# Transformer front end as a stream: modulation blocks grouped by chunk of h, first two projection blocks summed side by side

## What is computed

```python
sh1, sc1, g1, sh2, sc2, g2 = split(silu(cond) @ w_ada + b_ada, 6)   # 6 x 1024 for each of two conditions
h = rms_norm(x, norm1) * (1.0 + sc1) + sh1
z = h @ w_in                 # q | k | v | conv_in, 1792 wide
attn = attention(q, k, v)    # windowed, grouped heads, rotary, sink
conv = conformer_conv(u)     # GLU -> depthwise conv of 31 taps -> LayerNorm -> swish -> pointwise
x = x + g1 * (concat(attn, conv) @ w_out)
h2 = rms_norm(x, norm2) * (1.0 + sc2) + sh2
x = x + g2 * peer(h2)        # 16384 one-neuron experts, top 16 of each of 8 heads
```

## Time and profile before

| | |
|---|---|
| time, three runs | 1817.09 us median (1816.93 to 1817.82) |
| time of the profiled execution | 1817.6 us |
| its span, first to last instruction | 1815.6 us |
| mean granted clock of TensorE | 0.966 of full speed |
| TensorE matmul busy | 1692.0 us, 93% |
| VectorE busy | 1577.9 us, 87% |
| ScalarE busy | 767.1 us, 42% |
| GpSimd busy | 686.8 us, 38% |
| first part of the modulation and the norm, up to the first projection matmul | 0 to 38.3 us |
| input projection | 38.3 to 196.7 us |

### The profile page before, as it was taken

How to read it: one execution, slowest core, us unless ns; L and a number is a source line. 1 busy time by engine, 2 the same in 40 slices (tenths; PEclk the granted TensorE clock), 3 DMA queues, 4 the chain that set the end, 5 groups by cost and what they waited for, 6 DMA issues and landing times.

```text
span 1815.6 us, 28944 instructions
## 1 busy us (share of the span) xinstructions
PE 1692.0 (93%) x9360; PEld 1420.6 (78%) x9360; DVE 1577.9 (87%) x3181; ACT 767.1 (42%) x1653; POOL 686.8 (38%) x611
## 2 busy tenths in 40 slices
PE   6999988999963887799999999999999999999997
PEld 4566766955542787699989999998999999999986
DVE  2687852488889997799999999999999999999998
ACT  3122563330002888344444444444444444444443
POOL 0000000035565887344344444434343444444441
PEclk9999999999885999899999999999999999999999
DMA  8443102211112478999999999999999999999996
GB/s 318 140 142 137 47 1 73 70 59 58 35 35 93 140 228 256 367 398 388 392 405 400 400 401 398 414 390 394 408 406 395 409 393 404 404 410 399 394 392 211
DMA packets 128781, 508.71 MB, mean 280 GB/s; under 512 B 8528, under 2 KB 63568, under 8 KB 79312
## 3 DMA queue, kind: packets, MB, share of 16 engines
q0 software_dynamic: 36864, 268.45, 36.8%
q1 hardware_dynamic: 91568, 239.34, 35.2%
q10 hardware_dynamic: 288, 0.13, 0.0%
HBM read 479.97 MB, written 27.92 MB: 280 GB/s over the span
## 4 chain that ended last, share of the span: by engine, by line
DVE 35%; DMA 23%; PE 21%; issue 18%; POOL 1%; ACT 1%; DVEq 1%; POOLq 0%; SPq 0%; ACTq 0%
DMA slab<-table,ixr 21%; DVE slab L1452 8%; PE psum L413 7%; DVE ulo L1368 4%; PE psum L619 3%; DVE slab L1406 3%; DVE slab L1444 3%; PE psum L706 2%; DVE vlo L1431 2%; PE psum L414 2%; DVE slab L1439 2%; DVE wlo L1427 1%; POOL slab L1534 1%; PE psum L550 1%; DVE slab L1410 1%
## 5 line engine op out<-in xcount | busy, mean ns | idle before, releaser
L1534 POOL DMA_INDIRECT slab<-table,ixr x256 | 426.0, 1664 | 604.0 <-DVE slab L1452 554.3
L727 PE MATMUL psum<-hhi,uhi 128*128 128x384 f32 x1008 | 340.1, 337 | 7.4 <-issue 7.1
L1452 DVE SCALAR_TENSOR_TENSOR slab<-slab,cf 128x1024 f32<-128x1024 f32 x256 | 328.5, 1283 | 15.1 <-DVE slab L1452 0.5
L1444 DVE SCALAR_TENSOR_TENSOR slab<-slab,h2tok 128x1024 f32<-128x1024 f32 x256 | 312.3, 1220 | 33.5 <-DMA slab<-table,ixr 33.3
L727 PE MATMUL psum<-hhi,ulo 128*128 128x384 f32 x1008 | 339.0, 336 | 0.0
L727 PE MATMUL psum<-hlo,uhi 128*128 128x384 f32 x1008 | 338.5, 336 | 0.0
L741 PE MATMUL psum<-vhi,whi 128*128 128x512 f32 x768 | 299.6, 390 | 14.2 <-DVE wlo L1427 13.9
L741 PE MATMUL psum<-vhi,wlo 128*128 128x512 f32 x768 | 301.8, 393 | 0.0
L741 PE MATMUL psum<-vlo,whi 128*128 128x512 f32 x768 | 301.5, 393 | 0.0
L413 PE MATMUL psum<-slab 128*128 128x512 f32 x464 | 246.6, 614 | 7.9 <-ACT slab L862 5.2
L727 PEld LDWEIGHTS psum<-hhi,uhi 128*128 128x128 f32 x1008 | 190.0, 188 | 17.3 <-issue 12.8
(11 more groups left out here) (207 smaller groups left out, 2696.3 us busy)
## 6 DMA issues: line engine op xcount, KB each, us to landing
slab<-ublk SPq DMA_DIRECT2D x64, 1024.0 KB, 8.6
slab<-vtab SPq DMA_DIRECT2D x64, 1024.0 KB, 8.5
slab<-wblk SPq DMA_DIRECT2D x90, 512.0 KB, 4.1
slab<-g_dram SPq DMA_DIRECT2D x32, 768.0 KB
g_dram<-slab SPq DMA_DIRECT2D x11, 2048.0 KB, 7.5
slab<-table,ixr POOLq DMA_INDIRECT x256, 9.6
x<-x_in SPq DMA_DIRECT2D x1, 2560.0 KB, 9.4
y_out<-x SPq DMA_DIRECT2D x5, 512.0 KB, 3.5
```

What stands on the lines that cost most here:

```text
L727: last = pe.matmul(psum[:, b, 0:ND], w[:, c, :], m[:, c, :], start=(m_ == 0), stop=(m_ == 3 * DC - 1))
L1444: v.scalar_tensor_tensor(out=rows[:, sl % GR, 0:D], in0=rows[:, sl % GR, 0:D], scalar=1.0, in1=h2tok[:, k, :], op0=ALU.mult, op1=ALU.mult, ...
L1452: v.scalar_tensor_tensor(out=accs[k][:, e, :], in0=rows[:, sl % GR, D:2 * D], scalar=cf[:, sl:sl + 1], in1=accs[k][:, e, :], op0=ALU.mult, ...
L1534: pool.indirect_dma_start(out=rows[:, sl % GR, :], out_offset=None, in_=table, in_offset=bass.IndirectOffsetOnAxis(ap=ixr[:, half, sl % 8: ...
```

## The change

The 16 blocks of the first part of the modulation are laid out in another order: each group of four now holds the shift and the scale of two chunks of h (`pair_of` on the host). After three such groups come the first two projection blocks (seq 12 and 13), then the fourth group (14 to 17). All 18 have places of their own. The sum of squares is split: ScalarE squares two chunks at a time, VectorE adds the squares together, and TensorE sums over partitions once instead of eight times. VectorE and ScalarE make h by pairs of chunks as the groups come. The first two projection blocks are summed side by side: for each chunk of h, one piece of block 0 and one of block 1. The halves of the second part that stood behind the blocks 0 and 1 go behind the blocks 2 and 3, which have two halves each. The first four ring loads (seq 18 to 21) are issued together.

```diff
-S_ADA1, S_IN, S_PW, S_OUT, S_WQ, S_ADA3, S_END = 0, 16, 54, 58, 66, 82, 90
+S_PW, S_OUT, S_WQ, S_ADA3, S_END = 54, 58, 66, 82, 90
+GROUPS1 = N_ADA1 // ADA_G
+ADA_SEQ = (0, 4, 8, 14)
+IN_SEQ = (12, 13)
+TURN_BANK = (7, 6, 7, 4)
+N_LEAD = 18
...
+MID_HALVES = {2: (0, 1), 3: (2, 3), **{b: (b,) for b in range(4, N_HALF)}}
+MID_COPY = {2: 0, 3: 1, 5: 2, 7: 3, 9: 4, 11: 5}
+MID_TURN = {3: 0, 4: 1, 6: 2, 8: 3, 10: 4, 12: 5}
...
 def in_block(b):
-    return S_IN + b + ADA_H * min(b, N_HALF)
+    return IN_SEQ[b] if b < 2 else N_LEAD + b - 2 + ADA_H * sum(len(MID_HALVES.get(a, ())) for a in range(b))
...
-            for j in range(1, N_ADA1):
+            for j in range(1, N_LEAD):
                 sp.dma_start(lead[j], wblk[j]).then_inc(lead_in[j], 16)
-            for j in range(RING):
-                sp.wait_ge(blk_done, j + 1)
-                sp.dma_start(ring[:, j], wblk[S_IN + j]).then_inc(ring_in[j], 16)
+            sp.wait_ge(blk_done, ADA_G)
+            for at in range(N_LEAD, N_LEAD + RING):
+                sp.dma_start(ring[:, at % RING], wblk[at]).then_inc(ring_in[at % RING], 16)
...
-            load(S_IN + RING, S_OUT - S_IN - RING)
+            load(N_LEAD + RING, S_OUT - N_LEAD - RING)
...
-            for g in range(groups1):
-                ada(S_ADA1 + ADA_G * g, g)
-                if g == 0:
-                    pe.wait_ge(squares, 1)
-                    column_sum(h, DC, 0)
-                else:
-                    pe.wait_ge(row_copied, g)
-                    ada_turn(modrow[0][:, g - 1], 7, g - 1)
-            pe.wait_ge(row_copied, groups1)
-            ada_turn(modrow[0][:, groups1 - 1], 7, groups1 - 1).then_inc(ada_tp, 1)
+            def first_turn(g):
+                pe.wait_ge(row_copied, g + 1)
+                ada_turn(modrow[0][:, g], TURN_BANK[g], g).then_inc(ada_tp, 1)
+            def first_chunk(c):
+                pe.wait_ge(h_ready, c + 1)
+                for b in range(2):
+                    w = weights(IN_SEQ[b])
+                    last = both(lin[b], w[:, c, :], h[:, c, :], 0, T_L, c == 0, c == DC - 1)
+                    if c == DC - 1:
+                        last.then_inc(blk_done, 1)
+            ada(ADA_SEQ[0], 0)
+            pe.wait_ge(squares, 1)
+            both(stat, ones[:], h[:, 0, :], 0, T_L, True, True).then_inc(sums, 1)
+            first_turn(0)
+            ada(ADA_SEQ[1], 1)
+            first_turn(1)
+            pe.wait_ge(sums_read, 1)
+            ada(ADA_SEQ[2], 4)
+            pe.wait_ge(mod_set, 1)
+            first_turn(2)
+            for c in range(3):
+                first_chunk(c)
+            pe.wait_ge(mod_set, 2)
+            ada(ADA_SEQ[3], 6)
+            first_chunk(3)
+            first_turn(3)
+            for c in range(4, DC):
+                first_chunk(c)
...
             for b, (kind, _) in enumerate(IN_KINDS):
-                g = b // 2
-                if b >= 2:
-                    pe.wait_ge(lin_act, b - 1)
+                if b < 2:
+                    continue
+                pe.wait_ge(lin_act, b - 1)
...
-                if b < N_HALF:
-                    ada(half_block(b), 7, ADA_H * (b % 2), ADA_H * (b % 2 + 1))
+                for j, i in enumerate(MID_HALVES.get(b, ())):
+                    ada(half_block(b, j), 7, ADA_H * (i % 2), ADA_H * (i % 2 + 1))
...
-            act.activation(h, x[:], ACT.Square).then_inc(squares, 1)
+            for c in range(0, DC, 2):
+                act.activation(h[:, c:c + 2, :], x[:, c:c + 2, :], ACT.Square).then_inc(x_squared, 1)
...
-            for g in range(groups1):
-                copy_rows(S_ADA1 + ADA_G * (g + 1), modrow[0][:, g], g)
-                if g == groups1 - 2:
-                    act.wait_ge(inverse, 1)
-                    act.activation(rb[:, 0:N], rb[:, 0:N], ACT.Sqrt).then_inc(root, 1)
-            add_shift(0, M_SH1)
+            copy_rows(ADA_G, modrow[0][:, 0], 0)
+            copy_rows(2 * ADA_G, modrow[0][:, 1], 1)
+            act.wait_ge(inverse, 1)
+            act.activation(rb[:, 0:N], rb[:, 0:N], ACT.Sqrt).then_inc(root, 1)
+            add_shift(0, M_SH1, range(1))
+            copy_rows(3 * ADA_G, modrow[0][:, 2], 4)
+            add_shift(0, M_SH1, range(1, 6))
+            copy_rows(4 * ADA_G, modrow[0][:, 3], 6)
+            add_shift(0, M_SH1, range(6, DC))
...
+            for k in range(1, DC // 2):
+                v.wait_ge(x_squared, k + 1)
+                if k > 1:
+                    settle()
+                step(v.tensor_tensor(h[:, 0:2, :], h[:, 0:2, :], h[:, 2 * k:2 * k + 2, :], ALU.add))
+            settle()
+            v.tensor_tensor(h[:, 0, :], h[:, 0, :], h[:, 1, :], ALU.add).then_inc(squares, 1)
             inverse_mean(1, rb[:, 0:N], stat[:, 0:N], D)
-            read_mod(1, 7, N_ADA1, M_SH1)
-            norm_gain(0, M_SC1, V_NORM1)
-            rms_scale(0, 1)
+            for g in range(2):
+                read_pair(g)
+            rms_scale(0, 1, range(0, 4))
+            for g in range(2, 4):
+                read_pair(g)
+                rms_scale(0, 1, range(2 * g, 2 * g + 2))
```

More of the change, by code:

```diff
@@ L182, in build @@
         keyT = view(9216, SB, P)
-        lead = [view(5120 + 1024 * j, DC, P) for j in range(14)] + [view(21872 + 1024 * j, DC, P) for j in range(2)]
+        lead = [view(5120 + 1024 * j, DC, P) for j in range(12)] + [view(28016 + 1024 * j, DC, P) for j in range(2)] + [view(c0, DC, P) for c0 in (17408, 18432, 21872, 22896)]
         z = view(11264, QK, N)
@@ L245, in build @@
         mod_set = sem("mod_set"); row_copied = sem("row_copied"); ada_tp = sem("ada_tp"); blk_done = sem("blk_done")
-        squares = sem("squares"); sums = sem("sums"); sums_read = sem("sums_read"); inverse = sem("inverse"); root = sem("root"); piled = sem("piled")
+        squares = sem("squares"); sums = sem("sums"); sums_read = sem("sums_read"); inverse = sem("inverse"); root = sem("root"); piled = sem("piled"); x_squared = sem("x_squared")
         scaled = sem("scaled"); h_ready = sem("h_ready"); lin_act = sem("lin_act"); lin_dve = sem("lin_dve"); spread = sem("spread")
@@ L262, in build @@
         kv_stored = sem("kv_stored")
-        lead_in = [sem(f"lead_in{i}") for i in range(N_ADA1)]
+        lead_in = [sem(f"lead_in{i}") for i in range(N_LEAD)]
         ring_in = [sem(f"ring_in{i}") for i in range(RING)]
@@ L469, in rotate @@
                 pe.wait_ge(znorm, c + 1)
-                pe.wait_ge(mod_set, 1 + turns)
+                pe.wait_ge(mod_set, GROUPS1 + turns)
                 if c:
@@ L770, in _, with add_shift @@
         def _(act):
-            def add_shift(half, col):
-                for c in range(DC):
+            def add_shift(half, col, chunks=range(DC)):
+                for c in chunks:
                     act.wait_ge(scaled, DC * half + c + 1)
@@ L873, in out_lead @@
                 seq = S_OUT + j
[L874 removed]
+                act.wait_ge(ring_in[seq % RING], 16 * ((seq - N_LEAD) // RING + 1))
                 if j >= 2:
@@ L1066, in inverse_mean, with read_pair, rms_scale @@
                 v.reciprocal(r, r).then_inc(inverse, 1)
-            def rms_scale(half, root_k):
+            def read_pair(g):
+                v.wait_ge(ada_tp, g + 1)
+                pair = slice(2 * g, 2 * g + 2)
+                bias = V(V_BADA, 2 * DC).rearrange("p (s c) -> p s c", s=2)[:, :, pair].unsqueeze(3).broadcast_to([P, 2, 2, 2])
+                v.tensor_tensor(mod[:, 0:2 * DC, :].rearrange("p (s c) k -> p s c k", s=2)[:, :, pair, :],
+                                psum[:, TURN_BANK[g], 2 * ADA_G * g:2 * ADA_G * (g + 1)].rearrange("p (s c k) -> p s c k", s=2, c=2), bias, ALU.add).then_inc(mod_set, 1)
+                v.wait_ge(mod_set, g + 1)
+                step(v.scalar_tensor_tensor(out=gain[:, 0, :, pair], in0=mod[:, M_SC1 + 2 * g:M_SC1 + 2 * g + 2, :].rearrange("p c k -> p k c"), scalar=1.0,
+                                            in1=V(V_NORM1 + 2 * g, 2).unsqueeze(1).broadcast_to([P, 2, 2]), op0=ALU.add, op1=ALU.mult))
+                settle()
+            def rms_scale(half, root_k, chunks=range(DC)):
                 v.wait_ge(root, root_k)
-                for c in range(DC):
+                for c in chunks:
                     v.scalar_tensor_tensor(out=h[:, c, 0:T_L], in0=x[:, c, 0:T_L], scalar=gain[:, half, 0, c:c + 1], in1=rb[:, 0:T_L],
@@ L1630 @@
     win = blocks(a["win"][:, np.concatenate(order)])
-    front = []
-    for b in range(N_IN):
+    pair_of = [np.r_[2 * g:2 * g + 2, DC + 2 * g:DC + 2 * g + 2] for g in range(GROUPS1)]
+    front = [ada[pair_of[0]], ada[pair_of[1]], ada[pair_of[2]], win[0:2], ada[pair_of[3]]]
+    for b in range(2, N_IN):
         front.append(win[b:b + 1])
-        if b < N_HALF:
-            front.append(ada[N_ADA1 + ADA_H * b:N_ADA1 + ADA_H * (b + 1)])
-    wblk = np.concatenate([ada[:N_ADA1], *front, blocks(a["pw"]),
+        for i in MID_HALVES.get(b, ()):
+            front.append(ada[N_ADA1 + ADA_H * i:N_ADA1 + ADA_H * (i + 1)])
```

(1 more changed line is left out.)

59 lines of the change are left out of this document (29 added, 30 removed).

## The result

The changed kernel takes 1820.52 us (median of 20 runs, 1817.02 to 1826.26) against 1817.32 us of the kernel before (20 runs, 1814.84 to 1820.86): a ratio of 1.002, interval 1.0012 to 1.0028. It is 3 to 6 us slower, where a gain of 0.7 us was forecast.

The account below looks back on a forecast made before the run. TensorE's chain up to projection block 4 was taken as the bound: 50.5 us, plus 22.4 of work, 5.7 of ring stalls and 2.0 for the clock, gives 80.6 instead of 81.32; gain 0.7, so 1816.4 us, range 1812.5 to 1820.5.

Parts of the forecast that it names:

- the clock in the front: TensorE's clock falls by 30.2 us; the lower level costs 0 to 2.8 us, taken 2.0, so block 1 ends at 52.5.
- the second gap of the ring: Behind block 3, block 4's load (seq 28) lands 5.3 us after the block's end, stalling TensorE 2.3 us.
- The front without the clock: With the clock at its upper level, the first projection chunk starts at 30.2 us and blocks 0 and 1 end at 50.5.
- The ring: Behind blocks 2 and 3 TensorE waits for late ring loads: stalls of 3.4 and 2.3 us, 5.7 in all.
- The rival of the falls in the gaps: Ring gaps behind blocks 2 and 3 lower TensorE's clock, 2.1 us each: 1818.5 for one fall, 1820.6 for two; chance 0.2.
- VectorE's early gate is worth nothing: VectorE's first gate moves from 60.7 to about 54.6 us; the 6 us become a longer wait before 103.
- Ring waits hidden: Loads behind blocks 2 and 3 come early enough, saving the 5.7 us: 1810.7, or 1808.7 with the clock up; chance 0.1.

Follow-up runs that it names:

- e3: Changed kernel with three spare places for late ring blocks (seq 22, 23, 27, 28) and five filler matmuls in the front: 1807.86 us against 1817.94 for the kernel before.
- e2: Changed kernel with five filler matmuls of 512 columns in the front, into a bank nobody reads: 1819.03 us against 1817.94 for the kernel before.
- e4: Kernel before with only the halves behind blocks 0 and 1 moved behind blocks 2 and 3, front unchanged: 1827.42 us against 1817.94.
- e9: Changed kernel again, word for word, for a second timing and profile: 1823.29 us against 1817.39 for the kernel before.
- e1: Changed kernel with three spare places in SBUF for ring blocks seq 22, 23, 27 and 28, loaded early: 1809.04 us against 1817.94 for the kernel before.
- e7: Kernel before with only the sum of squares split (squares in four, additions on VectorE, one sum on TensorE): 1813.03 us against 1817.4.
- e10: e7 again, word for word: 1814.04 us against 1817.39 for the kernel before.
- e11: e7 with seven sums put back as idle work on TensorE ahead of the one real sum: 1814.95 us against 1817.04 for the kernel before.
- e12: e3 with only the first three of its five fillers, those in the wait for the squares: 1808.79 us against 1817.04 for the kernel before.

## Why the prediction was wrong

The prediction was 1816.4 us, a gain of 0.7, with 1812.5 to 1820.5 as its range; the two medians, 1820.52 and 1823.29, lie at and above its upper end. The mechanisms were named in the prediction. Two terms of its sum were too small, the clock in the front and the second gap of the ring, and a third, the falls of the clock in the gaps, was priced but left out of the sum.

- **The front without the clock: right within 0.8 us.** With the clock held up (e3) the first chunk starts at 30.91, predicted 30.2, and block 2 ends at 60.06, so both first blocks end at 51.3, predicted 50.5. The squares are ready at 19.1 (predicted 19.2). The 0.8 may be the fillers' own, which delay the sum by 1.0 in e3.
- **The step that failed first: "between 0 and 2.8, taken 2.0" for the clock.** The fall was predicted "by 30.2" and its cost counted only from the first dense matmul on. In the first profile it came at 20, at the one sum, and stretched both `ada` groups and three turns, which are on the chain in this order. Both first blocks end at 56.1 (block 2, 8.75 us long, ends at 64.9), 4.8 us after e3's 51.3. That is 2.8 more than the sum had. Against the predicted 52.5 both blocks end 3.6 us late.
- **The ring: right in kind, 5.7 in the sum, 7.3 and 6.1 us of waits measured.** Behind block 2 the count holds: 5.4 predicted from block end to block start, 5.2 measured (64.92 to 70.16). Behind block 3 it was 5.3 predicted, 7.3 measured (78.89 to 86.18). There the landing of seq 28 was taken as that of a load alone, 3.4 us. It was issued at 80.6, 1.7 us after the block's end (1.85 predicted), and took 5.4; that of 27 had been issued 1.4 us before it, and 29 to 31 followed at 81.1, 82.0 and 83.5 and took 6.2, 6.6 and 6.3. That its neighbours slowed it is argued and not shown: no run varies them. Rows with such lengths were at hand: 3.4 to 5.2 us for loads that follow each other.
- **The rival of the falls in the gaps, given 0.2 and left out of the sum.** The clock fell behind block 3 in both profiles of the changed kernel, and behind both blocks in e2 and e4: six of eight gaps. Its price in the first profile is the 2.7 us between the delay of block 4 (4.9) and that of the scores (7.6). The Trainium skill, page "TensorE: Matmul & The Clock Gate", section "HAM oscillation — how this bites in real kernels", had it that each burst behind a transfer wait starts cold; the traces agree in six gaps of eight, and not in the two behind block 2 of the changed kernel (granted clock 1.00 from 38 to 84 us in the first profile). That this rival's 1820.6 for two falls is nearly the first median is luck: only one of them occurred, and 3.6 us of the loss lay in the front.

By the first profile: gain 0.7, less 3.6 for the front and its clock and 2.0 for the second gap, is 4.9 us late at block 4; less 2.7 for the fall behind it, 7.6 at the scores. In e9's profile it is 2.5 and 4.2. The medians lie 3.2 and 5.9 over the kernel before.

- **VectorE's early gate is worth nothing: right.** It waited 11.3 us at the root sums, and 9.0 in e9.
- **"Ring waits hidden", given 0.1 for 1808.7 to 1810.7,** did not happen, but e1 and e3 made it happen and measured it: 1809.04 and 1807.86. Over the kernel before this is 4.7 and 7.9 us at the first scores, 8.9 and 10.1 by the medians. The ring's waits and the falls of the clock took more than all of it.

What stays open: why the split of the sum alone lowers the median by 2 to 4 us (e7, e10, e11) with a front that is no shorter in the profile; and how the share of the two losses splits in the executions without a profile.

## What to carry to other kernels

When blocks are moved in a fixed load order, count for each block which one it displaces in the ring and when that one is finished: four short blocks behind a long one, with a ring of four, put one transfer's whole latency on the chain. Removing dense matmuls from a stretch that waits for something else (weights, or another engine's result) gained nothing in e7's profile and can let TensorE's clock fall for what follows; look at what the removed work lay under, and at what runs next. When a forecast is a small difference between a gain and losses of like size, give each loss a bound of its own: here the gain was right within 0.8 us, and losses that were counted too low decided the sign.

## What the runs showed of the hardware

- TensorE's clock fell at 20 us behind 1.85 us of idle and one sum of 1.3 us (first profile; 1.94 us of idle in e1), as it had before behind turns and 2.75 us of idle. Three matmuls of 512 columns in that place kept it up (e12, 1.00 from 16 to 26 us). A turn takes 1.71 to 1.87 us at the lower level and 0.95 to 1.05 at the upper.
- In e9 the granted clock reads 1.00 from 20 to 28 us while the turn takes 1.71 us and the sum 2.07: the lengths of the lower level. The first change that the row shows is the fall near 33 us. The 16 `ada` matmuls at 16.64 took 1.08 us there, for 0.72 in the first profile, so the level was low by then and no fall is needed to explain the sum. The same stands in e4, where the first pair of the sums takes 1.75 us at 17.94, and in e11 (2.08 at 17.86), both under a granted clock of 1.00. That the level was low from the start of the execution is inferred. Up to the first change in the row the lengths of the instructions decide:

```profile
19.30 2.07 PE L427 MATMUL psum<-slab,ones 128*128 128x512 f32 x2 [1.58 <-DVE slab L1159]
...
21.59 1.71 PE L422 MATMUL psum<-con,slab 128*128 128x2 f32 x8
```

```profile
20.00:24.00 4.00, 4.00 (x28) 3.10 (x30) 2.13 (x2) 0.00 (x0) 0.00 (x0) 1.00 1.03 421
```

- A ring load of 512 KB that was issued into an idle queue (79.2 us) took 3.3 us from issue to landing. The next, issued 1.4 us later and with others behind it, took 5.4, and the ones after it 6.2 to 6.6.
